# A two-part transformer block on one core: products in pairs, half-row norms, three outputs at once, an earlier weight half

## The reference, cut to what matters

```
def _swiglu(x, w1, w3, w2):
    return (jax.nn.silu(x @ w1) * (x @ w3)) @ w2
...
    for l in range(DEPTH):
        h = _swiglu(x, ffn_w1[l, 0], ffn_w3[l, 0], ffn_w2[l, 0])
        x = _layernorm(ALPHA * x + 0.5 * h, ln_g[l, 0], ln_b[l, 0])
        ...
        x = _layernorm(ALPHA * x + h, ln_g[l, 1], ln_b[l, 1])
        h = _swiglu(x, ffn_w1[l, 1], ffn_w3[l, 1], ffn_w2[l, 1])
        x = _layernorm(ALPHA * x + 0.5 * h, ln_g[l, 2], ln_b[l, 2])
```

```
        mod = jax.nn.silu(c) @ w_mod[layer] + b_mod[layer]
...
        h = modulate(rmsnorm(x, norm1_g[layer]), sh1, sc1)
        hc = modulate(rmsnorm(ctx, norm1_g[layer]), sh1c, sc1c)
...
        v_g_c = heads(hc @ wv_g, GLA_HEADS)
...
    y = jax.nn.sigmoid(m_a) * (o_na @ w_br_na) + jax.nn.sigmoid(m_b) * (o_gla @ w_br_gla)
    return y @ w_o
...
        x = x + g1 * mix
        h2 = modulate(rmsnorm(x, norm2_g[layer]), sh2, sc2)
        x = x + g2 * swiglu(h2, w_ffn_gate[layer], w_ffn_up[layer], w_ffn_down[layer])
```

## Time and profile before

| | |
|---|---|
| median of 3 runs | 1785.64 us |
| lowest and highest run | 1783.6 and 1789.44 us |
| the profiled execution: its own time | 1787.88 us |
| the profiled execution: its span, first to last instruction | 1786.1 us |
| mean granted TensorE clock, share of full speed | 0.996 |

### The profile page before, as it was taken

The page is one execution under the profiler, slowest core; times in us unless marked ns, Lnnn a source line. Parts: engine busy times, 40 slices in busy tenths (PEclk is TensorE's granted clock), DMA queues, the critical chain, the costliest instruction groups (busy, mean ns, idle before and its releaser), DMA issues. The chain is left out here.

```text
span 1786.1 us, 31142 instructions
## 1 busy us (share of the span) xinstructions
PE 1759.3 (98%) x12755; PEld 1604.1 (90%) x12755; DVE 1142.4 (64%) x1803; ACT 864.1 (48%) x1412; POOL 217.7 (12%) x284
## 2 busy tenths in 40 slices
PE   9999999999999999999999999999999999999999
PEld 9998699999899879997899997999768877889999
DVE  5774667776777466656586876676647455655553
ACT  5453344664444435443446653545436355445543
POOL 2000122211000000001222211000003243200000
PEclk9999999999999999999999999999999999999999
DMA  8585666445667557755765456676435333356663
GB/s 294 190 271 181 218 220 222 143 151 195 198 211 259 190 192 234 235 189 163 263 214 189 139 179 215 200 259 209 148 128 134 92 95 105 119 164 190 191 198 107
DMA packets 257518, 334.71 MB, mean 187 GB/s; under 512 B 15210, under 2 KB 217168, under 8 KB 257376
## 3 DMA queue, kind: packets, MB, share of 16 engines
q1 hardware_dynamic: 251312, 317.42, 54.7%
q0 software_dynamic: 6064, 15.31, 2.7%
HBM read 327.45 MB, written 1.05 MB: 184 GB/s over the span
## 5 line engine op out<-in xcount | busy, mean ns | idle before, releaser
L1883 DVE TENSOR_TENSOR wlo<-raw,whi 128x1024 fp32r<-128x1024 f32 x549 | 670.8, 1228 | 351.4 <-ACT whi L1444 346.8
L1444 ACT ACTIVATE whi<-raw 128x1024 fp32r<-128x1024 f32 x549 | 572.7, 1051 | 419.1 <-PE bank L759 223.2
L733 PE MATMUL bank<-XTh,whi 128*128 128x256 f32 x1984 | 555.6, 280 | 0.0
L736 PE MATMUL bank<-XTh,wlo 128*128 128x256 f32 x1984 | 551.7, 278 | 0.0
L734 PE MATMUL bank<-XTl,whi 128*128 128x256 f32 x1984 | 551.4, 278 | 0.0
L733 PEld LDWEIGHTS bank<-XTh,whi 128*128 128x128 f32 x1984 | 373.5, 188 | 2.3
L736 PEld LDWEIGHTS bank<-XTh,wlo 128*128 128x128 f32 x1984 | 374.3, 189 | 0.5 <-DVE wlo L1883 0.4
L734 PEld LDWEIGHTS bank<-XTl,whi 128*128 128x128 f32 x1984 | 372.9, 188 | 0.0
L733 PE MATMUL bank<-HCh,whi 128*128 128x256 f32 (+2 forms) x880 | 251.8, 286 | 0.6 <-DVE tmp L2419 0.6
L734 PE MATMUL bank<-HCl,whi 128*128 128x256 f32 (+2 forms) x880 | 247.6, 281 | 0.0
L736 PE MATMUL bank<-HCh,wlo 128*128 128x256 f32 (+2 forms) x880 | 247.3, 281 | 0.0
(11 more groups left out here) (344 smaller groups left out, 2362.2 us busy)
## 6 DMA issues: line engine op xcount, KB each, us to landing
raw<-in_ffn_w_dram SPq DMA_DIRECT2D x131, 1024.0 KB, 5.2
raw<-in_w_in_dram SPq DMA_DIRECT2D x76, 1024.0 KB, 5.2
raw<-in_w_mod_dram SPq DMA_DIRECT2D x24, 1024.0 KB, 5.1
raw<-in_w_branch_dram SPq DMA_DIRECT2D x16, 1024.0 KB, 5.1
raw<-in_w_out_dram SPq DMA_DIRECT2D x12, 1024.0 KB, 4.9
raw<-in_w_ffn_gate_dram SPq DMA_DIRECT2D x11, 1024.0 KB, 5.1
raw<-in_w_ffn_up_dram SPq DMA_DIRECT2D x11, 1024.0 KB, 5.0
raw<-in_w_ffn_down_dram SPq DMA_DIRECT2D x8, 1024.0 KB, 5.0
```

The costliest lines, as they stand in the source:

```text
L733: e.matmul(o, hi[:, k, w0:w0 + nc_], xh, start=first and k == 0, stop=False)
L736: m = e.matmul(o, lo[:, k, w0:w0 + nc_], xh, start=False, stop=last and k == nk - 1)
L1444: e.activation(hi_part(n), raw_part(n), ACTF.Copy).then_inc(WHI.did(n), 1)
L1883: e.tensor_tensor(lo_part(n), raw_part(n), hi_part(n).bitcast(F32), ALU.subtract).then_inc(WLO.did(n), 1)
```

## The change

Five things are changed.

- `x_bank` gives banks 0 to 3 after norms 0 and 3 (before: 0, 1, 2, 7), and `row_bank` puts the modulation row of these norms in bank 6 instead of 3.
- DVE's `layernorm` is cut up. The last scale-and-shift works by half rows (512 columns), each with a signal of its own, and PE's `turn_x` waits for each half. The first addition of t = 1 moves ahead of the last scaling of t = 0. At norms 0 and 3 one `low_x` moves ahead of the last scaling of t = 1, and at norm 5 the first low weight part (`w.more(1)` in `scale`). Two low weight parts come before the remaining `low_x`.
- `gemm_pair` runs the first two up products together, phase by phase, so that low x is needed after 32 matmuls, not after 16.
- `start` in `gemm_b` does the same for the two held parts of V.
- `first_three` computes the first three outputs of the output projection together: k = 0 to 5 in three phases over all three, then k = 6, 7 of each.

```
 def x_bank(s, t, c):
-    return (0, 1, 2, 7)[2 * t + c] if s % 3 == 1 else 4 + 2 * t + c
+    return 2 * t + c + (0 if s % 3 == 1 else 4)
+def row_bank(j):
+    return 6 if j % 3 == 0 else 3
...
+            def gemm_pair(outs, X, coming):
+                held = [w.take() for _ in outs]
+                for n, o in zip(held, outs):
+                    for k in range(8):
+                        coming(k, XHI)
+                        q.wait_ge(WHI, n)
+                        e.matmul(o, hi_part(n)[:, k, :], X(k)[0], start=k == 0, stop=False)
+                for n, o in zip(held, outs):
+                    q.wait_ge(WLO, n)
+                    for k in range(8):
+                        e.matmul(o, lo_part(n)[:, k, :], X(k)[0], start=False, stop=False)
+                for n, o in zip(held, outs):
+                    for k in range(8):
+                        coming(k, XLO)
+                        m = e.matmul(o, hi_part(n)[:, k, :], X(k)[1], start=False, stop=k == 7)
+                    w.give_back()
+                    m.then_inc(MM.did(("w", n)), 1)
...
+                def start(held, ti):
+                    t = tiles[ti]
+                    for p, n in enumerate(held):
+                        ready(p, t, XHI)
+                        q.wait_ge(WHI, n)
+                        for c in range(nb):
+                            if p == 0:
+                                empty(banks[ti][c])
+                            e.matmul(bank[banks[ti][c]][:, :], X(p, t)[0], hi_part(n)[:, 0, c * 512:(c + 1) * 512], start=p == 0, stop=False)
+                    for p, n in enumerate(held):
+                        q.wait_ge(WLO, n)
...
+                    for p, n in enumerate(held):
+                        ready(p, t, XLO)
...
+                    if s:
+                        q.wait_ge(DLN, ("x", s - 1, t, c))
...
-                    q.wait_ge(DLN, ("x", j, 0))
                     turn_x(j + 1, 0)
-                modulation_half(g, h, True, True)
+                modulation_half(g, h, True, True, row_bank(j))
...
             def layernorm(j, gbn, turn=True):
+                def scale(t):
+                    if t and not turn:
+                        w.more(1)
+                    q.wait_ge(PLN, ("rs", j, t))
+                    q.wait_ge(DLN, ("g", j, t))
+                    for c in range(2):
+                        xv = X[:, t, c * 512:(c + 1) * 512]
+                        e.scalar_tensor_tensor(xv, xv, rs[:, t, 1:2], gb[:, 1, c * 512:(c + 1) * 512], ALU.mult, ALU.add).then_inc(
+                            DLN.did(("x", j, t, c), ("x", j, t)), 1)
+                for c in range(2):
+                    add(0, c)
+                    stats(0, c)
+                center(0)
+                add(1, 0)
+                scale(0)
+                stats(1, 0)
+                add(1, 1)
+                stats(1, 1)
+                center(1)
+                if j % 3 == 0:
+                    low_x(j + 1, 0, 0)
+                scale(1)
                 w.more(1)
                 w.take_whole()
...
+                def first_three():
+                    held = [w.take() for _ in range(3)]
+                    outs = [bank[(32 + i) % 3][:, 0:T] for i in range(3)]
+                    for i in range(3):
+                        empty((32 + i) % 3)
+                    for product in (high, low_weight, low_y):
+                        for n, o in zip(held, outs):
+                            for k in range(6):
+                                product(n, o, k)
+                    for i, (n, o) in enumerate(zip(held, outs)):
+                        for product in (high, low_weight, low_y):
+                            for k in (6, 7):
+                                m = product(n, o, k)
+                        w.give_back()
```

More of the change, by code:

```diff
@@ L853, in modulation_half @@
                     kk = 4 * h + k
-                    m = e.matmul(bank[3][0:2, :], csil[:, kk, :], raw_whole(c)[:, k, :], start=kk == 0, stop=last and k == 3)
+                    m = e.matmul(bank[b][0:2, :], csil[:, kk, :], raw_whole(c)[:, k, :], start=kk == 0, stop=last and k == 3)
                 m.then_inc(MOD.did(("whole", c), ("mod", g, h)), 1)
                 if last:
-                    emptied[3] = ((AMD, ("row", g, h)),)
+                    emptied[b] = ((AMD, ("row", g, h)),)
             def mod_columns(g, b):
@@ L1497, in layernorm @@
                 w.take_whole()
-                mod_row(*NORMS[j])
+                mod_row(*NORMS[j], row_bank(j))
                 if turn:
```

96 lines of the change are left out of this document (61 added, 35 removed).

## The result

| | before | changed |
|---|---|---|
| median | 1786.12 us (4 runs) | 1772.11 us (4 runs) |
| lowest and highest | 1783.6 and 1789.44 us | 1770.63 and 1776.25 us |
| ratio, with its 95% interval | | 0.9924 (0.99 to 0.9948) |
| profiled execution: time, span, mean clock | 1787.88, 1786.1, 0.996 | 1771.4, 1769.7, 0.999 |

The changed kernel is faster by 0.76%, 14 us by the medians. A second set of six executions gave 1773.41 us and the ratio 0.9929 (0.9909 to 0.9949). I predicted 1775.5 us, a gain of some 10.

A forecast was written before the change was run, and what follows sets the result against it. TensorE, in flight 1759.3 of 1786.1 us, bounds the kernel. Terms 2.3 + 2.2 + 0.8 - 0.2 - 1.2 + 6.7 + 0.6 sum to 11.2 us: 1776.7, taken as 1775.5 us; 8-in-10 range 1768.5 to 1782.5.

The forecast's parts named there:

- Norms 2, 4 and 1: Transposes and up products behind these norms: PE's waits for DVE go, gaining 2.3, 2.2 and 0.8 us.
- Norm 5 and vg: Value weights' low parts after norm 5: 3.4 us less wait, 3.4 from a vanished clock fall; sum 6.7 us.
- My remaining wait of 0.65: After norm 5, PE would still wait 0.65 us for the second low part, and not for the fourth.
- The early subtraction: After norm 5, DVE's subtraction behind the centering would not hold up POOL's inverse root; at most 0.4 us hangs on it.
- The clock: At V's waits in both layers, falls of 1.7 us each charged at about 0.7 for the two: 1.2 us lost.
- rival 1: No fall of the clock at the new waits: gain 15.1 us, time 1771.6 us (chance 0.18).
- The output projection: Three outputs together: PE waits 3.1 us for the third bank, the clock falls, 0.6 us gained; without a fall 2.3.
- V and the matrices: After norms 0 and 3, PE starts V earlier but waits longer for the causal matrices, 2.7 and 2.0 us: gain 0.
- no net term: Stretches may turn between slow and fast pace, 2.6 to 3.3 us each after norms 1 and 4; nothing net was counted.
- My sign of being wrong: Among the signs in the changed profile: more than some 800 matmuls change their pace.
- Rival 4: Waits released by another engine may set a slow pace, 4.5 ns a matmul: slower, 1805 us at most (chance 0.03).
- Rivals 2 and 3: Second block takes its gain back, 1779 to 1782 us (chance 0.2); up products fail too, 1780.5 us (chance 0.07).

The follow-up runs named there:

- changed, again: The changed kernel, unaltered, profiled and timed a second time: median 1773.41 us over six executions, ratio 0.9929 to the kernel before.
- no pair: The changed kernel with the first two up products one after the other as before: median 1782.02 us, ratio 0.9976 to the kernel before.
- one transpose: The changed kernel with the first two up products one after the other and one extra transpose behind them: 1784.9 us, ratio 1.0002 to before.

## Why the prediction came out as it did

Each stage in the three traces, from mark to mark on PE, with its slow matmuls:

| stage up to | before | changed | changed, again |
|---|---|---|---|
| transposes of norm 0 | 195.93 (396) | 197.64 (435) | 195.93 (403) |
| causal matrices | 22.61 | 21.88 | 21.67 |
| norm 1 | 233.09 (919) | 231.76 (612) | 231.89 (657) |
| norm 2 | 192.72 (0) | 192.48 (23) | 192.25 (29) |
| norm 3 | 194.37 (561) | 189.90 (4) | 189.89 (4) |
| causal matrices | 23.16 | 21.71 | 22.63 |
| norm 4 | 231.81 (661) | 231.78 (645) | 230.00 (260) |
| modulation of norm 5 | 194.94 (21) | 192.94 (3) | 196.32 (768) |
| transposes of `CX` | 23.13 | 16.58 | 16.59 |
| end | 474.38 | 473.00 | 476.73 |

- **Norms 2, 4 and 1.** Predicted 2.3, 2.2 and 0.8 us; measured 2.09, 1.97 and 0.56. The mechanism was right, with waits gone where I had them gone. The norm by halves and the pair share it, and need each other: from the transposes to the end of the pair at norm 2 it takes 13.71 us before, 13.31 without the pair but with the new norm, 12.52 with the pair and the norm of before, 11.62 with both.
- **Norm 5 and vg.** Predicted 6.7, measured 6.55: 3.2 us of waits and 3.4 of the fall at 1301. My remaining wait of 0.65 was 0.47. The early subtraction did not hold up POOL's root: it took 1.52 us in both traces. But my reading of the earlier trace rows was wrong. There the root ended at 286.05, 0.42 us behind the end of the subtraction beside it; in all 14 traces every root of a norm ended 0.40 to 0.45 us behind the end of the DVE instruction that ran when it started. After norm 5 that is the centering, and the subtraction starts behind it, so the root waits no longer than before. The rule that GpSimd contends with VectorE instructions of two SBUF inputs (the Trainium skill, GPSIMD Engine Reference, "Key points") agrees with these rows; the 0.4 us that I had worked out from it for this place did not appear. Here the fall was no rare one: it came in all three traces with both waits (6.83, 3.41 and 3.41 us), and in none of the eleven others.
- **The clock.** I charged falls to waits by their length, and counted two falls where the trace has a third, at 1448 behind the wait of 2.15 us. In the 14 traces the wait of 3.1 us was followed by a fall in 6 of 9, the wait of 2.15 us at 1432 in 12 of 14. At these two places it is a chance per execution. My rival 1, no fall at the new waits, was the profiled execution; its 1771.6 is near the 1771.4 measured, but partly by luck of the pace. Over all executions the change gives back 1.8 us of clock (13.0 us by the means, 11.2 at full clock).
- **The output projection.** The 3.1 us wait and its cause, the third bank, were right. The gain of 0.6 with a fall on both sides was near (0.1 to 0.45 by the order alone); the profile's 1.7 is the fall that was not drawn.
- **The failed step: V and the matrices.** I took 0 for the waits and -1.2 for the clock, since PE would only wait longer (2.7 and 2.0 us). It waited 1.81 and 0.33. The stages became shorter by 0.7 and 1.45 us, and by 0.9 and 0.5 in the second trace. POOL's masking started 20.73 and 20.54 us behind the norm's first transposes, where it was 21.45 and 21.11: 0.7 and 0.6 us earlier. The norm's new order accounts for some 0.8 us in the first layer and 0.2 in the second (means over nine traces with it, 20.7 and 20.8, and over three without, 21.6 and 21.0); the rest is scatter, from 20.1 to 22.0. The other 0.9 us of the second layer is the masking's own length, 1.12 for 2.00, which is luck: it was 2.11 in the second trace. And PE was ready for the matrices only 1.4 and 0.2 us earlier behind those transposes, not 1.8 and 0.6. The new start of V was not tested by itself. No fall came there in either trace of the changed kernel; one came in three of the twelve others, behind waits of 2.3 to 3.9 us.
- **The failed step: the pace.** "I take no net term." The pair has one. With it, the stretch behind norm 2 was fast in all of ten traces, and slow in the three without it and without thin matmuls (before, no pair, one transpose). Behind norm 1 it was slow in none of ten with it and in two of those three. Behind norm 4 it stays chance: slow in five of ten. The profiled gain has 707 fewer slow matmuls (836 fewer in the stages above, some 130 more behind them), 3.2 us, of which 2.5 behind norm 2. My sign of being wrong, more than some 800 that change, can't decide: stretch by stretch some 1,900 changed, but between the two traces of the changed kernel some 2,100 did. Rival 4 had the right price (117.8 against 113.3 ns) and the wrong sign. Its mechanism, a wait that sets the pace, is not borne out: with thin matmuls added the waits stayed and the pace turned. Rivals 2 and 3 did not happen: nothing won is paid back in the second block (its stage keeps 1.4 us more). The Trainium skill (TensorE: Matmul & The Clock Gate, "Back-to-back issue gap") gives one isolated gap, 109 ns for 256 columns; the stretches here ran at 113 or 118 ns.
- **The sum, again.** It had 11.2 us; the profiled spans are 16.4 apart. V and the matrices gave 3.4 more than I had (2.2 of stages, 1.2 of clock), the pace 3.2, the projection 1.2, and the norms and vg 0.9 less. The first stage took 1.7 us longer (I had 0.2), 0.63 of it a wait for a low weight part at 92.3; in the second trace it took 195.93, as before, so I take it for chance. That 1775.5 was only 3.4 us off the median is partly luck, since the errors of the terms cancel in part.

What sets the pace inside TensorE is not settled. Shown is that a stretch has its pace within its first some 20 matmuls and keeps it for 384 to 1,188 of them, but for pieces of 20 to 50, and that it can be turned by instructions that do no work: thin matmuls and a transpose gave the fast pace at all but one place, a transpose alone did not. It is not fixed by the program: with the same instructions ahead of it, the stretch behind norm 4 was at either pace.

## What to carry to other kernels

Read the pace (starts per 10 us at clock 1.00) as well as the waits: on a path that is 98% TensorE, a stretch at 118 ns instead of 113 costs as much as three waits of a microsecond, and an edit at its entry can turn it. Price a fall of the clock as a chance times 1.7 or 3.4 us, from several traces, not as a certainty behind a wait of a given length. When outputs are computed together, wait for each one's bank at its own first matmul, and issue loads that have no need to wait ahead of those that do.

## What the hardware did unexpectedly

- The same program ran the stretch behind norm 4 with 3 slow matmuls in one execution and 768 in the next, 3.4 us apart, at clock 1.00.
- The clock fell behind a wait of 2.15 us in 12 of 14 traces and behind one of 3.1 in 6 of 9, twice some 1 us before that wait ended. Ahead of the last microseconds of a run, each fall lasted 3.41 us (24 of them) or 6.83 (10). In 7 of 14 it also fell once between 1323 and 1337 us, behind no wait over 1.02 us, and once right behind 24 thin matmuls.
- A float32 matmul of two columns is two instructions of 0.11 us each.
- POOL's masking of 128x1024 took 1.10 to 2.11 us, and the difference is DVE's: in the 14 traces it ended 0.96 us behind the end of the subtraction that was running when it started (16 times), and took 1.10 where none was running, even when one started during it (12 times). With the landing of its loads this set PE's wait anywhere between 0.3 and 3.9 us.
